# Reading expert weights in 8 KB runs per partition, with the contraction rows dealt out in another order

## The chip, the core and the metric

The kernel runs on one core of one Trainium2 chip. The metric is the device time of one execution in microseconds, as a median of runs.

## The reference, cut to what matters

One encoder layer on 2048 tokens of width 1024: attention and pooling, then a mixture of experts, then a final norm. The change touches the mixture of experts alone. There are 128 routed experts and one shared expert, each with a hidden width of 256; every token goes to 8 routed experts and to the shared one. All weights are float32.

```python
def swiglu(h, wg, wu, wd):
    return (jax.nn.silu(h @ wg) * (h @ wu)) @ wd        # wg, wu: 1024 x 256, wd: 256 x 1024

    def expert_block(args):                             # one block: 128 rows of one expert
        tok, rw, e = args
        xs = hp[tok]
        y = swiglu(xs, w_gate_e[e], w_up_e[e], w_down_e[e])
        return (y.astype(jnp.float32) * rw[:, None]).astype(hf.dtype)
```

The result of each block is added to the rows of its tokens.

## The kernel before, in words

The first part (up to about 950 us) works through 16 tiles of 128 tokens: norm, projection, attention, pooling, router. It writes the normed rows to a table in DRAM (`h2_tab`) and, for each expert, a list of (token, weight) records (`rec_tab`). A short stage then makes tables of the blocks: which records block b has, which expert it belongs to, and at which blocks the weights of the next expert are to be split. The second part is the expert loop. It has 16 blocks for the shared expert and some 200 for the routed ones. A last part norms the 2048 rows and stores them.

In the expert loop each engine has its own instruction stream, written out by hand, and they meet only at semaphores. `EW` is 6144, the columns of one expert's weights in a partition: `GUW` = 4096 for gate and up, 2048 for down. `KD` is 8, the number of 128-row slices of the contraction of 1024.

SP loads weights (`load`, L366 to L382), for one expert after another. `RAW` has two slots. For expert m, SP first waits until the gate and up weights of expert m-1 have landed (L404) and until VectorE has split those of m-2 (L406), then issues the loads of gate (L378) and up (L379). In the same way it waits for the down weights of m-1 (L409) and the split of those of m-2 (L411) and issues the load of down (L381). Each of the three loads has 1 MB. Contraction row k*128+p lies in partition p. A run that is contiguous in both DRAM and SBUF is one row: 1 KB for gate and up, which are interleaved slice by slice in `RAW`, and 4 KB for down.

ScalarE and VectorE split the weights into a float32r upper part and the remainder, six pieces of 1024 columns an expert (`upper` L577 with the copy on L586, `lower` L874 with the subtraction on L887), from `RAW` into `WS`, which also has two slots. That is done one expert ahead of TensorE.

GpSimd (POOL, L480 to L495) does three things in each block, all on one DMA queue, the software queue q0: it waits for the release of a row buffer (`xg_used`) and for the records of an earlier issue (L486), gathers the 128 rows of the block four ahead (`gather`, L461: 128 rows of 4 KB), waits for VectorE's result and for the previous addition (L488, L490), adds the finished block to `acc_tab` (L492: 128 rows of 4 KB, an accumulating DMA), and issues the load of the records of the block six ahead (`load_rec`, L478: 128 records of 8 bytes). The wait on L486 counts every record load issued so far, so that the gather of an iteration begins only when the record load issued at the end of the iteration before has landed. The hardware queue of SP is q1.

TensorE (L1073 to L1099) does, in each block b: gate and up (`parts` L1065 with `KD` = 8: 24 matmuls of 512 columns, L1068 to L1070, stationary `XR`), once the split weights and the split rows are there; 8 transposes of the rows of block b+1 (L1086, the helper's line is L956); the first half of the down projection of block b-1 (6 matmuls, stationary `HR`), once VectorE has emptied the output banks (L1088) and split the hidden rows (L1089); two transposes of the hidden block (L1097) once `hb` is there (L1095); and the other 6 down matmuls. In a transpose the data to be transposed is the stationary operand, which LDWEIGHTS reads, and the identity is the moving one.

VectorE in each block: the product `hb` (L908), the lower half of the rows (L894), the gate and up pieces of the next expert if they are due (L887), then, after `y_done` and the landing of the addition two blocks back (L914), the scaled result (L917), the lower half of the hidden rows (L921), and the down pieces. There are two result buffers, `ys`. ScalarE: silu (L608), the upper half of the rows (L590), pieces (L586), the upper half of the hidden rows (L616).

Of the kernel before, what the change touches and what calls it, by code (L numbers as in the profile page):

```python
# [6 lines left out]
P = 128  # L7
T = 2048
D = 1024
KD = D // P  # L10
# [19 lines left out]
EW = 6144  # L30
SLOTS = 2
UNROLL = 8
AHEAD = 4
# [3 lines left out]
GUW = 4096  # L37
# [73 lines left out]
def build(nc, A, out):  # L111
# [4 lines left out]
    with ctx:  # L116
# [17 lines left out]
        ident = C("ident")  # L134
# [97 lines left out]
        B = [PB[:, n, :] for n in range(8)]  # L232
# [9 lines left out]
        s = {n: sem(n) for n in names}  # L242
# [39 lines left out]
        RAW = over("RAW", SLOTS * EW, 0)  # L282
        WS = over("WS", 2 * SLOTS * EW, SLOTS * EW, f32r)
        WSf = WS[:, :].bitcast(f32)
        xg = [arena[:, 36864 + n * D:36864 + (n + 1) * D] for n in range(AHEAD)]
# [21 lines left out]
        def _(sp):  # L307
# [58 lines left out]
            def load(m, slot, part):  # L366


                at = slot * EW
                if isinstance(m, int) and m == 0:  # L370
                    src = lambda name: A[{"gate": "w_sh_gate", "up": "w_sh_up", "down": "w_sh_down"}[name]][0].rearrange("(k p) n -> p k n", p=P)
                else:
                    e = sp.value_load(tab[0:1, bass.ds(m + (9 * P - 1), 1)] if not isinstance(m, int) else tab[0:1, 9 * P + m - 1:9 * P + m],
                                      min_val=0, max_val=E - 1)
                    src = lambda name: A[f"w_{name}_e"][0, bass.ds(e, 1)].rearrange("a (k p) n -> p (a k) n", p=P)
                if part == "gu":
                    guv = RAW[:, at:at + GUW].rearrange("p (k a n) -> p k a n", k=KD, a=2)
                    sp.dma_start(guv[:, :, 0, :], src("gate")).then_inc(s["w_gu"], 16)  # L378
                    sp.dma_start(guv[:, :, 1, :], src("up")).then_inc(s["w_gu"], 16)  # L379
                else:  # L380
                    sp.dma_start(RAW[:, at + GUW:at + EW].rearrange("p (k n) -> p k n", k=2),  # L381
                                 src("down")).then_inc(s["w_dn"], 16)  # L382

            sp.wait_ge(s["p_proj"], NT)
            load(0, 0, "gu")
# [558 lines left out]
        def _(pe):  # L944
# [9 lines left out]
            def transposes(banks, src, name):  # L954
                for k in range(KD):
                    last = tr(B[banks[k // 4]][:, (k % 4) * P:(k % 4 + 1) * P], src[:, k * P:(k + 1) * P], ident)  # L956
                last.then_inc(s[name], 1)

            def step(i):
                if ok(i + 1):  # L960
                    W8(pe, "v_xn", i + 2)
# [98 lines left out]
            nblk = pe.value_load(nblk_i[0:1, 0:1], min_val=NT + 1, max_val=NT + 255)  # L1060
            pe.sem_inc(s["gu_done"], 1)
            pe.wait_ge(s["xg_r0"], 16)
            transposes((2, 3), xg[0], "xg_used")

            def parts(bank, hi, lo, w, K):  # L1065

                for k in range(K):
                    mm(bank, hi[:, k, :], w(k, 0), start=(k == 0), stop=False)  # L1068
                    mm(bank, hi[:, k, :], w(k, EW), start=False, stop=False)  # L1069
                    last = mm(bank, lo[:, k, :], w(k, 0), start=False, stop=(k == K - 1))  # L1070
                return last

            with pe.Fori(0, (256 + NT) // UNROLL) as q:  # L1073
                with pe.If(q * UNROLL < nblk + 1):
                    for n in range(UNROLL):
                        b = pe.snap(q * UNROLL + n)
                        with pe.If(b < nblk + 1):
                            l1 = pe.value_load(tab[0:1, bass.ds(b + (3 * P + 1), 1)], min_val=0, max_val=E)
                            at = pe.snap((l1 & 1) * (2 * EW))
                            pe.wait_ge(s["v_spg"], l1 + 1)  # L1080
                            pe.wait_ge(s["xgT_a"], b * 2 + 2)
                            pe.wait_ge(s["xgT_v"], b * 2 + 2)
                            parts(B[7], xh, xl, lambda k, o: WS[:, bass.ds(at + (o + k * 512), 512)], KD).then_inc(s["gu_done"], 1)
                            m = n + 1
                            pe.wait_ge(s[f"xg_r{m % AHEAD}"], (q * (UNROLL // AHEAD) + (m // AHEAD + 1)) * 16)
                            transposes((2, 3), xg[m % AHEAD], "xg_used")  # L1086
                            l0 = pe.value_load(tab[0:1, bass.ds(b + 3 * P, 1)], min_val=0, max_val=E)
                            pe.wait_ge(s["y_v"], b + 1)  # L1088
                            pe.wait_ge(s["hT_sb"], b + 1)  # L1089
                            pe.wait_ge(s["v_spd"], l0 + 1)  # L1090
                            at0 = pe.snap((l0 & 1) * (2 * EW))
                            down_w = lambda c: lambda k, o: WS[:, bass.ds(at0 + (o + GUW + k * D + c * 512), 512)]
                            parts(B[4], hh, hl, down_w(0), 2)

                            pe.wait_ge(s["h_ready"], b + 1)  # L1095
                            for k in range(2):
                                tr(B[6][:, k * P:(k + 1) * P], hb[:, k * P:(k + 1) * P], ident)  # L1097
                            parts(B[5], hh, hl, down_w(1), 2).then_inc(s["y_done"], 1)
                    settle(pe)  # L1099

# [23 lines left out]
```

## Time and profile before

| what | value |
|---|---|
| median of 3 runs | 3520.7 us (3518.12 to 3538.77) |
| profiled execution, from the first to the last instruction | 3472.9 us |
| first part, table stage and start of the loop | 0 to about 1130 us |
| routed blocks of the expert loop | about 1130 to 3400 us, 198 iterations of POOL |
| TensorE busy, share of the span | 85% |
| VectorE, ScalarE, GpSimd busy | 62%, 49%, 27% |
| bytes moved by DMA | 730 MB, mean 210 GB/s |

The profile is of one execution; its span is 47.8 us below the median of the runs, for what lies around the instructions and for the difference between executions. Busy is the time in which an engine has an instruction at work. A DMA load is cut into packets, which 16 DMA engines work off; a queue's share is the time that its packets took, as a share of 16 engines' time in the stretch.

### The profile page before, as it was taken

To read this page: it belongs to the slowest core of one execution; us is meant where nothing else is said; L and a number is where in the kernel's file an instruction comes from. 1 tells how busy PE (TensorE), PEld (TensorE's weight loads), DVE (VectorE), ACT (ScalarE), POOL (GpSimd) and SP (SyncE) were. 2 spreads that over 40 slices of the span, in tenths; PEclk is the share of its full clock that TensorE was granted. 3 is DMA by queue.
4 is the path that set the end of the run, shared out by engine and by line. 5 is a ranking of instruction groups with operands and counts; after the bars stand their busy time and mean duration, and the time that the engine had idled before them with its cause. 6 is when DMAs were issued, how large, how long until landed. Compare 5 with 4: busy or idle time off the path is not lost.

```text
span 3472.9 us, 61999 instructions
## 1 busy us (share of the span) xinstructions
PE 2951.9 (85%) x13151; PEld 2180.6 (63%) x13152; DVE 2164.1 (62%) x3443; ACT 1706.3 (49%) x2435; POOL 925.5 (27%) x794
## 2 busy tenths in 40 slices
PE   6699999999469989888798888888888888998883
PEld 2355555555358877776676767676767667776662
DVE  1146666666643665667676766666766675667774
ACT  0133333333133654656565655556556565656565
POOL 0001111111223333232333333333332323333331
PEclk9899999999779999999899999999999999999896
DMA  9501111111175887989998999899989998899997
GB/s 368 163 25 49 49 48 36 49 36 43 67 182 122 239 228 208 269 260 259 289 295 252 290 281 274 258 271 285 288 259 265 265 293 232 247 266 280 294 275 249
DMA packets 415300, 730.08 MB, mean 210 GB/s; under 512 B 31521, under 2 KB 297377, under 8 KB 414754
## 3 DMA queue, kind: packets, MB, share of 16 engines
q1 hardware_dynamic: 341314, 500.17, 42.5%
q0 software_dynamic: 73824, 228.47, 28.6%
q14 instruction: 149, 1.22, 0.1%
q8 instruction: 13, 0.21, 0.0%
HBM read 587.37 MB, written 141.19 MB: 210 GB/s over the span
## 4 chain that ended last, share of the span: by engine, by line
DMA 45%; PE 22%; issue 12%; DVE 8%; POOL 7%; POOLq 4%; ACT 2%; DVEq 0%; SPq 0%; ACTq 0%
DMA rec<-rec_tab 42%; PE PB L986 8%; POOL arena L461 3%; POOL acc_tab L492 3%; POOLq L476 3%; PE PB L951 2%; PE PB L1068 2%; PE PB L1070 2%; PE PB L1069 2%; DMA arena<-in_ada_b 1%; PE PB L1045 1%; PE PB L956 1%; DMA acc_tab<-arena,rec 1%; PE PB L970 1%; PE PB L1011 1%
## 5 line engine op out<-in xcount | busy, mean ns | idle before, releaser
L887 DVE TENSOR_TENSOR WS<-RAW,WS (+1 forms) x774 | 900.8, 1219 | 127.3 <-ACT WS L586 125.3
L586 ACT CAST WS<-RAW (+1 forms) x774 | 759.5, 1052 | 153.2 <-DMA RAW<-in_w_up_e 99.6
L1068 PE MATMUL PB<-WS,XR 128*128 x1720 | 685.6, 399 | 52.2 <-issue 46.6
L461 POOL DMA_INDIRECT arena<-h_tab,rec x219 | 255.3, 1166 | 1574.7 <-DMA rec<-rec_tab 1381.1
L1070 PE MATMUL PB<-WS,XR 128*128 x1720 | 674.7, 392 | 0.0
L1069 PE MATMUL PB<-WS,XR 128*128 x1720 | 674.0, 392 | 0.0
L917 DVE SCALAR_TENSOR_TENSOR arena<-PB,rec,G 128x512 f32<-128x512 f32 x430 | 302.5, 745 | 383.7 <-DMA acc_tab<-arena,rec 336.5
L1068 PE MATMUL PB<-WS,HR 128*128 x860 | 402.9, 468 | 154.1 <-DVE HR L921 153.0
L492 POOL DMA_INDIRECT acc_tab<-arena,rec x215 | 402.5, 1872 | 93.3 <-issue 68.4
L1068 PEld LDWEIGHTS PB<-WS,XR 128*128 128x128 f32 x1720 | 327.6, 190 | 158.7 <-issue 91.8
L1069 PEld LDWEIGHTS PB<-WS,XR 128*128 128x128 f32 x1720 | 326.7, 190 | 66.1
L1070 PEld LDWEIGHTS PB<-WS,XR 128*128 128x128 f32 x1720 | 325.4, 189 | 67.6
L1070 PE MATMUL PB<-WS,HR 128*128 x860 | 363.4, 423 | 0.0
L1069 PE MATMUL PB<-WS,HR 128*128 x860 | 361.6, 420 | 0.0
L956 PE MATMUL PB<-cst,arena 128*128 128x128 f32 x1984 | 265.4, 278 | 97.3 <-DVE arena L814 53.1
L449 POOL DMA_INDIRECT rec_tab<-recs,posi x128 | 124.6, 973 | 795.5 <-DVE recs L748 754.8
L956 PEld LDWEIGHTS PB<-cst,arena 128*128 128x128 f32 x1984 | 235.8, 143 | 138.2 <-DVE arena L814 48.4
L894 DVE TENSOR_TENSOR XR<-PB,XR 128x512 fp32r<-128x512 f32 x432 | 277.6, 684 | 65.0 <-ACT XR L590 64.8
L608 ACT ACT_TABLE_LOAD x215 | 275.8, 1283 | 74.4 <-issue 70.5
L1068 PEld LDWEIGHTS PB<-WS,HR 128*128 128x128 f32 x860 | 176.4, 205 | 193.0 <-issue 169.4
L986 PE MATMUL PB<-arena 128*128 128x512 f32 (+1 forms) x768 | 293.7, 544 | 1.5 <-ACT arena L515 1.2
L590 ACT ACTIVATE XR<-PB 128x512 fp32r<-128x512 f32 x432 | 234.6, 595 | 98.3 <-PE PB L956 98.3
(233 smaller groups left out, 2982.6 us busy)
## 6 DMA issues: line engine op xcount, KB each, us to landing
RAW<-in_w_gate_e SPq DMA_DIRECT2D x128, 1024.0 KB
RAW<-in_w_up_e SPq DMA_DIRECT2D x128, 1024.0 KB
RAW<-in_w_down_e SPq DMA_DIRECT2D x128, 1024.0 KB, 8.6
arena<-in_ada_w SPq DMA_DIRECT2D x12, 2048.0 KB, 14.3
arena<-in_x SPq DMA_DIRECT2D x32, 512.0 KB, 3.6
h_tab<-arena SPq DMA_DIRECT2D x17, 512.0 KB, 2.9
acc_tab<-arena SPq DMA_DIRECT2D x16, 512.0 KB, 2.6
out<-fa SPq DMA_DIRECT2D x16, 512.0 KB, 4.7
```

The costliest lines, as they stand in the source:

```text
L461: g.indirect_dma_start(xg[n % AHEAD], None, h2_tab, bass.IndirectOffsetOnAxis(ap=rec[:, n % UNROLL, 0:1], axis=0)).then_inc(s[f"xg_r{n % A ...
L492: g.indirect_dma_start(acc_tab, bass.IndirectOffsetOnAxis(ap=rec[:, (n - 1) % UNROLL, 0:1], axis=0), ys[(n - 1) % 2], None, compute_op=ALU ...
L586: nc.scalar.copy(to, of).then_inc(s["a_hig" if k < 4 else "a_hid"], 1)
L608: A_(eg, B[7][:, 0:F], ACT.Silu).then_inc(s["eg_done"], 1)
L887: last = V.tensor_tensor(lo, raw, hi, ALU.subtract)
L894: V.tensor_tensor(xl[:, 4 * n:4 * n + 4, :], B[2 + n].rearrange("p (a b) -> p a b", a=4), xhf[:, 4 * n:4 * n + 4, :], ALU.subtract).then_i ...
L917: last = V.scalar_tensor_tensor(out=ys[(n - 1) % 2][:, c * 512:(c + 1) * 512], in0=B[4 + c], scalar=recf[:, (n - 1) % UNROLL, 1:2], in1=G2 ...
L956: last = tr(B[banks[k // 4]][:, (k % 4) * P:(k % 4 + 1) * P], src[:, k * P:(k + 1) * P], ident)
L986: last = mm(B[4 + n][:, 0:w], xT[:, k, :], w_in[:, k, n * 512:n * 512 + w], start=(k == 0), stop=(k == KD - 1))
L1068: mm(bank, hi[:, k, :], w(k, 0), start=(k == 0), stop=False)
L1069: mm(bank, hi[:, k, :], w(k, EW), start=False, stop=False)
L1070: last = mm(bank, lo[:, k, :], w(k, 0), start=False, stop=(k == K - 1))
```

## The change

The contraction rows are dealt to partitions in another order: partition p holds rows 8p to 8p+7 of gate and up (before: rows p, 128+p, 256+p and so on), and rows 2p and 2p+1 of down. So a partition's share of each of the three weights is one contiguous run of 8 KB in DRAM. In `RAW` and `WS` gate and up no longer alternate slice by slice: all of gate comes first, then all of up. A gate and up matmul reads its 512 moving columns as two runs of 256 that lie 2048 columns apart. The split into pieces is the same code on the same number of columns.

The stationary operands must have their rows in the same order. The transposes of the gathered rows take, for slice k, columns k, k+8, k+16 and so on (a step of 32 bytes), by a new helper `row_transposes`; the two transposes of the hidden block take every other column (a step of 8 bytes).

```diff
--- before.py
+++ after.py
@@ -368,18 +368,16 @@
 
                 at = slot * EW
                 if isinstance(m, int) and m == 0:
-                    src = lambda name: A[{"gate": "w_sh_gate", "up": "w_sh_up", "down": "w_sh_down"}[name]][0].rearrange("(k p) n -> p k n", p=P)
+                    src = lambda name: A[{"gate": "w_sh_gate", "up": "w_sh_up", "down": "w_sh_down"}[name]][0].rearrange("(p k) n -> p (k n)", p=P)
                 else:
                     e = sp.value_load(tab[0:1, bass.ds(m + (9 * P - 1), 1)] if not isinstance(m, int) else tab[0:1, 9 * P + m - 1:9 * P + m],
                                       min_val=0, max_val=E - 1)
-                    src = lambda name: A[f"w_{name}_e"][0, bass.ds(e, 1)].rearrange("a (k p) n -> p (a k) n", p=P)
+                    src = lambda name: A[f"w_{name}_e"][0, bass.ds(e, 1)].rearrange("a (p k) n -> p (a k n)", p=P)
                 if part == "gu":
-                    guv = RAW[:, at:at + GUW].rearrange("p (k a n) -> p k a n", k=KD, a=2)
-                    sp.dma_start(guv[:, :, 0, :], src("gate")).then_inc(s["w_gu"], 16)
-                    sp.dma_start(guv[:, :, 1, :], src("up")).then_inc(s["w_gu"], 16)
+                    sp.dma_start(RAW[:, at:at + GUW // 2], src("gate")).then_inc(s["w_gu"], 16)
+                    sp.dma_start(RAW[:, at + GUW // 2:at + GUW], src("up")).then_inc(s["w_gu"], 16)
                 else:
-                    sp.dma_start(RAW[:, at + GUW:at + EW].rearrange("p (k n) -> p k n", k=2),
-                                 src("down")).then_inc(s["w_dn"], 16)
+                    sp.dma_start(RAW[:, at + GUW:at + EW], src("down")).then_inc(s["w_dn"], 16)
 
             sp.wait_ge(s["p_proj"], NT)
             load(0, 0, "gu")
@@ -956,6 +954,13 @@
                     last = tr(B[banks[k // 4]][:, (k % 4) * P:(k % 4 + 1) * P], src[:, k * P:(k + 1) * P], ident)
                 last.then_inc(s[name], 1)
 
+            def row_transposes(src):
+
+                cols = src.rearrange("t (p k) -> t k p", k=KD)
+                for k in range(KD):
+                    last = tr(B[2 + k // 4][:, (k % 4) * P:(k % 4 + 1) * P], cols[:, k, :], ident)
+                last.then_inc(s["xg_used"], 1)
+
             def step(i):
                 if ok(i + 1):
                     W8(pe, "v_xn", i + 2)
@@ -1060,7 +1065,7 @@
             nblk = pe.value_load(nblk_i[0:1, 0:1], min_val=NT + 1, max_val=NT + 255)
             pe.sem_inc(s["gu_done"], 1)
             pe.wait_ge(s["xg_r0"], 16)
-            transposes((2, 3), xg[0], "xg_used")
+            row_transposes(xg[0])
 
             def parts(bank, hi, lo, w, K):
 
@@ -1080,10 +1085,11 @@
                             pe.wait_ge(s["v_spg"], l1 + 1)
                             pe.wait_ge(s["xgT_a"], b * 2 + 2)
                             pe.wait_ge(s["xgT_v"], b * 2 + 2)
-                            parts(B[7], xh, xl, lambda k, o: WS[:, bass.ds(at + (o + k * 512), 512)], KD).then_inc(s["gu_done"], 1)
+                            gu_w = lambda k, o: WS[:, bass.ds(at + o, GUW)].rearrange("p (a k n) -> p k a n", a=2, k=KD)[:, k]
+                            parts(B[7].rearrange("p (a n) -> p a n", a=2), xh, xl, gu_w, KD).then_inc(s["gu_done"], 1)
                             m = n + 1
                             pe.wait_ge(s[f"xg_r{m % AHEAD}"], (q * (UNROLL // AHEAD) + (m // AHEAD + 1)) * 16)
-                            transposes((2, 3), xg[m % AHEAD], "xg_used")
+                            row_transposes(xg[m % AHEAD])
                             l0 = pe.value_load(tab[0:1, bass.ds(b + 3 * P, 1)], min_val=0, max_val=E)
                             pe.wait_ge(s["y_v"], b + 1)
                             pe.wait_ge(s["hT_sb"], b + 1)
@@ -1094,7 +1100,7 @@
 
                             pe.wait_ge(s["h_ready"], b + 1)
                             for k in range(2):
-                                tr(B[6][:, k * P:(k + 1) * P], hb[:, k * P:(k + 1) * P], ident)
+                                tr(B[6][:, k * P:(k + 1) * P], hb.rearrange("t (p k) -> t k p", k=2)[:, k, :], ident)
                             parts(B[5], hh, hl, down_w(1), 2).then_inc(s["y_done"], 1)
                     settle(pe)
```

## Rows read from the trace of the kernel before

**Rows 1.** Windows by stage: time, busy us and count per engine, granted clock, DMA share, GB/s.

```profile
280.00:1130.00 850.00, 732.59 (x3261) 469.02 (x3261) 517.64 (x1256) 278.26 (x524) 173.58 (x174) 0.92 0.23 67
1600.00:2000.00 400.00, 345.27 (x1561) 274.48 (x1560) 280.04 (x351) 242.65 (x314) 136.20 (x102) 0.93 0.96 283
2000.00:2400.00 400.00, 347.93 (x1596) 278.30 (x1594) 269.56 (x342) 239.53 (x313) 128.68 (x103) 0.95 0.93 273
```

**Rows 2.** The page, the chain that ended last, shares by line.

```profile
DMA rec<-rec_tab 42%; PE PB L986 8%; POOL arena L461 3%; POOL acc_tab L492 3%; POOLq L476 3%; PE PB L951 2%; PE PB L1068 2%; PE PB L1070 2%; PE PB L1069 2%; DMA arena<-in_ada_b 1%; PE PB L1045 1%; PE PB L956 1%; DMA acc_tab<-arena,rec 1%; PE PB L970 1%; PE PB L1011 1%
```

**Rows 3.** Waits in 1130 to 3400 us: us in total, times, longest us.

```profile
POOL arena L461 <- DMA rec<-rec_tab: 1315.5, 176, 10.1
...
DVE arena L917 <- DMA acc_tab<-arena,rec: 335.3, 88, 9.3
...
PE PB L1068 <- DVE HR L921: 153.0, 58, 8.2
...
POOL arena L461 <- DVE arena L917: 118.2, 18, 8.1
...
ACT WS L586 <- DMA RAW<-in_w_up_e: 99.6, 22, 8.2
```

**Rows 4.** Counts in 1130 to 3400 us: the record load L478 and pieces L887.

```profile
L478 POOL DMA_DIRECT2D rec<-rec_tab x198: 1165/1226/1250, 1133.2 to 3394.0; - x198
...
L887 DVE TENSOR_TENSOR WS<-RAW,WS x762: 1209/1219/1294, 1137.7 to 3382.9; - x191
```

**Rows 5.** Timeline of POOL: start us, us, what [idle before <-releaser].

```profile
2007.31 1.77 POOL L461 DMA_INDIRECT arena<-h_tab,rec  x1 [8.53 <-DMA rec<-rec_tab]
...
2019.92 1.55 POOL L461 DMA_INDIRECT arena<-h_tab,rec  x1 [7.29 <-DMA rec<-rec_tab]
...
2193.20 0.98 POOL L461 DMA_INDIRECT arena<-h_tab,rec  x1 [8.69 <-DMA rec<-rec_tab]
...
2202.09 1.04 POOL L461 DMA_INDIRECT arena<-h_tab,rec  x1 [4.91 <-DMA rec<-rec_tab]
```

**Rows 6.** Timeline of PE, the first and tenth of a run of matmuls.

```profile
2000.34 0.39 PE L1068 MATMUL PB<-WS,XR 128*128 x1
...
2002.38 0.39 PE L1068 MATMUL PB<-WS,XR 128*128 x1
```

**Rows 7.** DMA queues in 1130 to 3400 us: packets, MB, share of 16 engines.

```profile
q1 hardware_dynamic: 294144, 393.76, 52.0%
q0 software_dynamic: 63360, 207.86, 39.3%
```

**Rows 8.** DMA queues in 1994.5 to 1997.5 us, gate and up alone.

```profile
q1 hardware_dynamic: 1068, 1.08, 106.9%
```

**Rows 9.** DMA queues in 2018.5 to 2020.4 us, down alone.

```profile
q1 hardware_dynamic: 177, 0.72, 100.6%
```

**Rows 10.** DMA queues in 30.5 to 33.5 us, 8 KB rows stored to rec_tab.

```profile
q1 hardware_dynamic: 173, 1.29, 101.5%
```

**Rows 11.** DMA queues in 1998.4 to 1999.4 us, a gather beside gate and up.

```profile
q0 software_dynamic: 72, 0.29, 77.0%
q1 hardware_dynamic: 85, 0.09, 25.9%
```

**Rows 12.** DMA queues in 2002 to 2004.5 us, an addition beside down.

```profile
q0 software_dynamic: 85, 0.35, 69.5%
q1 hardware_dynamic: 88, 0.32, 34.8%
```

**Rows 13.** Weight loads of transposes (L956) and matmuls (L1070) in 1130 to 3400 us, ns min/median/max.

```profile
L956 PEld LDWEIGHTS PB<-cst,arena x1584: 138/140/148, 1134.0 to 3395.4; 128*128 128x128 f32 x198
...
L1070 PEld LDWEIGHTS PB<-WS,XR x1584: 187/188/334, 1130.4 to 3399.5; 128*128 128x128 f32 x198
```

**Rows 14.** Timeline, eight weight loads of transposes in a row.

```profile
2004.87 1.02 PEld L956 LDWEIGHTS PB<-cst,arena 128*128 128x128 f32 x8
```

## The prediction

> **What bounds the kernel now.** I read the windows by stage first. In the expert loop (from about 1130 us) the 16 DMA engines are busy 93 to 96% of the time, against 23% in the first part [rows 1]. TensorE shows busy for 345 of 400 us there, so two resources are near their limit. The change touches only this loop, so the rest (about 1200 us of the span of 3472.9) stays as it is.
>
> Next the chain that ended last. Its largest share, 42% of the span, is the landing of the record load, a transfer of 1 KB [rows 2]. Such a small thing can take 42% only because of where it stands. It is the last entry that POOL puts on queue q0, behind a gather and an addition of 512 KB each, and the next gather waits until it has landed. The waits say the same: POOL's gather waited for the record load 176 times in 198 iterations, 1315.5 us in all, and only 18 times for VectorE [rows 3]. So POOL's loop mostly bounds itself: issue, drain q0, landing, issue. The others follow: VectorE waits 335.3 us for the landing of an addition, and TensorE 153.0 us for VectorE after it [rows 3].
>
> Then the length of that loop. 198 iterations between 1133.2 and 3394.0 us make 11.48 us each [rows 4]. When few weights are coming in, an iteration takes 8.89 us (2193.20 to 2202.09); beside a whole expert's load it takes 12.61 us (2007.31 to 2019.92) [rows 5]. The excess over the short iteration is 2.59 us, 510 us over 197 iterations. 762 pieces are 127 experts [rows 4], so the excess is 4.0 us for each expert loaded. That is what the change can act on.
>
> TensorE's floor lies close below. Ten starts in a row are 2.04 us apart for nine matmuls, 0.227 us each [rows 6]; 36 of them are 8.2 us, and eight transposes take 1.0 us [rows 14], two more 0.2 us, so about 9.4 us a block. 11.48 - 9.4 is 2.1 us of slack a block, 410 us over the loop. No gain can be larger.
>
> **The change part by part.**
>
> *The loads on their own.* A load of gate, up and down gives each DMA engine 128 packets of 1 KB and 16 of 4 KB; after the change 24 of 8 KB. Time for one packet: 1 KB, 3.0 us x 16 x 1.069 / 1068 = 48 ns [rows 8]; 4 KB, 1.9 x 16 x 1.006 / 177 = 173 ns [rows 9]; 8 KB, 1.29 MB are 157 packets, 3.0 x 16 x 1.015 / 157 = 310 ns [rows 10]. The last row is of stores from SBUF to DRAM; I take it for loads as well. Alone, a load is then 128 x 48 + 16 x 173 = 8.9 us now and 24 x 310 = 7.4 us after. In the loop the 125 loads took 52.0% of 2270 us, 9.44 us each [rows 7], 6% more than alone; the same 6% gives 7.9 us. So 1.5 us less DMA work an expert, 190 us over 127 experts. It isn't 190 us of time, since POOL's loop is bound by latency: q0 needs 39.3% of 2270 us over 198 blocks, 4.5 us [rows 7], in an iteration of 8.89, and weights that come in while q0 has nothing to move cost nothing.
>
> *What a load costs POOL's loop.* Now 4.0 us for 9.44 us of work, a share of 0.42. With the same share, 7.9 us cost 3.35 us: 0.65 us less for each of 127 experts, -83 us.
>
> *Turns.* Does the share stay? Where both queues have work, they take turns packet by packet: beside a gather 72 packets of q0 against 85 of q1 [rows 11], beside an addition 85 against 88 [rows 12]. With 1 KB packets q0 gives away 48 ns a turn and has 77% of the engines' time; against 4 KB it has 69.5%, with its own packets near 0.33 us (2.5 x 16 x 0.695 / 85). Against 8 KB it gives away 310 ns a turn, and its 16 data packets an engine in each block may each wait that long. Bounds: in one short iteration q0 leaves 8.89 - 4.5 = 4.4 us in which weights cost nothing. If all of that is used, a load confined to one iteration costs 7.9 - 4.4 = 3.5 us, and one spread over 1.55 iterations (197 / 127) costs 7.9 - 6.8 = 1.1 us. If turns let weights run early so that only 3.1 us fall into q0's pauses (my estimate, 70% of the 4.4 us), it costs 4.8 us. So between 1.1 and 4.8 us, against 4.0 now: -370 to +100 us. I take 3.35 us, since 3.5 is the bound nearest to the contested iteration of rows 5, and since a queue of 128 small packets, which q0 now finds ahead of it, becomes one of 16.
>
> A rule speaks against the change here. The Trainium skill, page "DMA: Bandwidth & Descriptors", section "Queues, rings and completion order", says that an engine goes round its queues and switches only at packet boundaries, and the section "SWDGE vs HWDGE vs iDMA" prefers packets of at most 4096 B. The trace agrees on the turns [rows 11, 12]; no row shows two queues beside 8 KB packets. By the rule the 8 KB packet costs q0 its full length in each turn, which is the rival priced at +100 us below.
>
> *The transposes.* Eight weight loads a block now read with a step of 32 bytes, two with a step of 8. Before, each takes 138 to 148 ns [rows 13] and eight take 1.02 us [rows 14]. No weight load of the trace has a step. Below, nothing changes (0; nothing excludes it, and a gain has no cause). Above, I take the slowest weight load of this shape in the loop, 334 ns [rows 13], at 194 ns more: 8 x 0.194 = 1.55 us a block, 307 us over 198. I take +1.0 us a block for the eight, a little above the middle of the two ends, since a step can hardly gain anything, and nothing for the two. The floor rises from 9.4 to 10.4 us, still below POOL's iteration of about 11.1, so most of it lies in time in which TensorE would wait (2.1 us a block). It shows where TensorE catches up after a late load; I charge one block in seven, 198 / 7 x 1.0 = +28 us. If that cover is gone, it is 198 us.
>
> The Trainium skill, page "Advanced Engine Details and Errata", section "Memory Cachelines", says that SBUF has lines of 16 bytes and that full bandwidth needs at least two hits a line. A step of 32 bytes has one hit, a step of 8 has two. No run here shows it yet. By that rule eight transposes slow down and two don't; by rows 13 and 14 alone nothing is known of either.
>
> *Gate and up's moving columns* in two runs of 256: each run is contiguous and the count is the same, 0; a step in the middle could cost a few ns of 227, with an upper end of 0.02 us x 24 a block, 95 us, that I hold unlikely. *The split* (L586, L887): same pieces, 0. *SP*: the same three issues an expert; it waits for landings that come earlier. The weights arrive some 1.5 us sooner. ScalarE waited 99.6 us in 22 waits for them [rows 3]; 22 x 1.0 us of it go, -20 us.
>
> **The sum.** -83 + 28 - 20 = -75 us on the profiled execution (3472.9 to about 3398), and from the median of the runs 3520.7 - 75 = 3445 us, 2.1% faster. What is late next is still the record load.
>
> **The rivals.**
> 1. *q0 starves (slower).* Each turn costs q0 a whole 8 KB packet, and a load costs POOL's loop 4.8 us instead of 4.0: 127 x 0.8 = +100, with +28 for the transposes: 3649 us at most, and I put it at 3560 to 3649. For it: turns are packet by packet [rows 11, 12], and POOL waits for q0 in 176 of 198 iterations [rows 3]. Against: a load then finishes sooner, within one iteration. It decides once the cost of a load passes 4.0 us.
> 2. *The transposes bind (slower or level).* With +1.0 us a block fully on the path, -83 - 20 + 198: 3616 us; with half of that, 3517. For it: the DMA-bound slack is only 2.1 us a block and shrinks as loads get cheaper. Against: TensorE waits for others in most long blocks [rows 3].
> 3. *It helps more.* The excess of a load falls to 2 us: 127 x 2.0 = -254, with +50 as the floor of 10.4 us is now felt: 3317 us. For it: 4.4 us of pause in an iteration take up most of 7.9 us. Against: loads come in bursts.
> 4. *Hidden anyway.* Shorter loads are used up by longer turns, 3505 to 3540 us: loads that end sooner only wait for the split.
>
> **How the numbers follow.** The forecast (3365 to 3485) has 0.43, rival 1 has 0.17, rival 2 has 0.12 (of it 0.04 level), rival 3 has 0.10, rival 4 has 0.18. A measurement of this kernel tells about 1% (35 us) from no change. Faster by over 1%: 0.43 + 0.10 = 0.53; slower: 0.17 + 0.08 = 0.25; within 1%: 0.22. For 8 in 10 the range goes from 3350 to 3590. The forecast's own range is 3365 to 3485.
>
> **What would show the steps.** Packets of 8192 B on q1, about 49,000 in place of 294,144 in the loop, and q1's time there down from 9.44 to about 7.9 us an expert. POOL's iteration down from 11.48 to about 11.1 us, with the record load still its main releaser. Eight transposes at 2.0 us instead of 1.02 us, with the pair on L1097 unchanged. Beside a gather q0's share falls from 77% to about 35%. The forecast is wrong if POOL's iteration doesn't get shorter although q1 is cheaper (rivals 1 and 4), if TensorE's waits vanish and its block goes beyond 10.4 us (rival 2), or if the packets stay small.

## The result, and the profile after

The changed kernel takes 3617.0 us (median of 3 runs, 3601.34 to 3622.75) against 3520.7 us before. The ratio is 1.0253, with an interval of 1.0193 to 1.0312: the change makes the kernel 2.5% slower. The forecast was 2.1% faster, 3445 us, with a range of 3350 to 3590 us. Medians below are of all executions of a kernel; ratios leave out those in which the chip shows a lower granted clock and a longer time.

Its profiled execution has a span of 3615.3 us, 142.4 us more than that of before. Of these the first part took 53 us: the first gather of the loop starts at 1015.0 us, before at 962.0 us (e1 below shows that this belongs to the one execution). First the windows by stage (columns as in [rows 1]):

```profile
1600.00:2000.00 400.00, 336.69 (x1530) 269.60 (x1528) 270.60 (x342) 241.74 (x313) 123.47 (x100) 0.96 0.87 276
2000.00:2400.00 400.00, 343.98 (x1528) 278.33 (x1529) 264.27 (x336) 225.05 (x294) 121.42 (x102) 0.93 0.84 260
```

The DMA engines are less busy than before, 84 to 87% instead of 93 to 96%, and still the same stretch gets less done: TensorE shows 1530 matmuls in 1600 to 2000 us, before 1561. So work was taken off the DMA engines, and the time went up.

The queues in the expert loop say the same (1130 to 3400 us, columns as in [rows 7]):

```profile
q1 hardware_dynamic: 51407, 374.36, 42.9%
q0 software_dynamic: 61440, 201.56, 40.1%
```

q1 has 51,407 packets instead of 294,144, and its share is 42.9% instead of 52.0%. 374.36 MB are 119.0 experts of 3.146 MB, so an expert takes 0.429 x 2270 / 119.0 = 8.18 us of the 16 engines, before 9.43 us. The saving was real: 1.25 us an expert, as a difference of the two shares.

The chain that ended last has the record load at its head as before (37%, before 42%), and the landing of the addition has grown to 5% (before 1%, [rows 2]):

```profile
DMA rec<-rec_tab 37%; PE PB L991 8%; DMA acc_tab<-arena,rec 5%; POOL arena L459 3%; PE PB L1073 2%; POOL acc_tab L490 2%; PE PB L1075 2%; PE PB L1074 2%; POOLq L474 2%; PE PB L949 2%; DMA arena<-in_ada_b 1%; PE PB L1050 1%; PE PB L1016 1%; PE PB L975 1%; PE PB L961 1%
```

The waits in 1130 to 3400 us (us in total, times, longest us), to be set beside [rows 3]:

```profile
POOL arena L459 <- DMA rec<-rec_tab: 1118.3, 142, 12.8
DVE arena L915 <- DMA acc_tab<-arena,rec: 461.0, 117, 11.4
...
POOL arena L459 <- DVE arena L915: 334.6, 43, 12.0
...
PE PB L1073 <- DVE HR L919: 182.3, 79, 5.7
...
ACT WS L584 <- DMA RAW<-in_w_up_e: 45.3, 13, 5.3
```

VectorE's wait for the landing of an addition went from 335.3 to 461.0 us, and the longest single wait of POOL for a record from 10.1 to 12.8 us. In total POOL waits less for the record (1118.3 us, before 1315.5), but more for VectorE: 334.6 us in 43 waits instead of 118.2 us in 18. I read this as VectorE, held up by a late addition, being late for the next one. Both together are 7.6 us an iteration (192 gathers), before 7.2 (198). The wait of ScalarE for weights fell, from 99.6 to 45.3 us; the weights do land sooner.

The record loads and the pieces of the loop (count, ns min/median/max, first and last start), to be set beside [rows 4]. The stretch here is 1130 to 3560 us, since this loop ends later:

```profile
L476 POOL DMA_DIRECT2D rec<-rec_tab x206: 1169/1226/1255, 1132.9 to 3553.7; - x103
```

```profile
L885 DVE TENSOR_TENSOR WS<-RAW,WS x762: 1205/1216/1271, 1190.9 to 3517.3; - x191
```

2420.8 us over 205 iterations are 11.81 us each, before 11.48. 762 pieces are the same 127 experts. The excess over the short iteration of 8.89 us is 2.92 x 205 / 127 = 4.7 us an expert, before 4.0. With 0.7 x 127 that is about 90 us in the loop. The medians differ by 96 us; the spans of the two profiles differ by these 90 and the 53 of the first part.

What the two queues do when they meet is in short stretches. First a gather beside 8 KB packets (2208 to 2210 us), then an addition beside them (2970 to 2972 us); columns as in [rows 11, 12]:

```profile
q1 hardware_dynamic: 84, 0.56, 66.1%
q0 software_dynamic: 70, 0.29, 34.8%
```

```profile
q0 software_dynamic: 52, 0.21, 53.1%
q1 hardware_dynamic: 51, 0.42, 51.6%
```

The packets still alternate one for one, 84 (of which 16 are the small ones that end a load) against 70, and 51 against 52. But the share of q0 beside a gather is 34.8%, where it was 77.0% [rows 11], and beside an addition 53.1%, where it was 69.5% [rows 12].

Last, the weight loads of the transposes, with a step of 32 bytes (L961) and of 8 bytes (L1103) in the changed kernel, and eight of the former in a row on the timeline:

```profile
L961 PEld LDWEIGHTS PB<-cst,arena x1544: 186/191/208, 1130.8 to 3392.9; 128*128 128x128 f32 x193
```

```profile
L1103 PEld LDWEIGHTS PB<-cst,arena x386: 194/196/228, 1133.0 to 3394.5; 128*128 128x128 f32 x193
```

```profile
2206.18 1.09 PEld L961 LDWEIGHTS PB<-cst,arena 128*128 128x128 f32 x8
```

The former took 138 to 148 ns before [rows 13]; the latter had this row in the kernel before:

```profile
L1097 PEld LDWEIGHTS PB<-cst,arena x396: 137/140/229, 1136.3 to 3397.0; 128*128 128x128 f32 x198
```

Each got some 50 ns longer, but eight in a row take 1.09 us instead of 1.02 [rows 14].

The moving columns in two runs cost nothing. The gate and up matmuls of 1130 to 3400 us, before and after:

```profile
L1068 PE MATMUL PB<-WS,XR x1585: 387/389/791, 1130.2 to 3399.9; 128*128 x199
```

```profile
L1073 PE MATMUL PB<-WS,XR x1544: 387/389/791, 1129.6 to 3399.5; 128*128 x193
```

The median is 389 ns in both, and a piece of the split takes 1216 ns, before 1219. The mean granted clock is a little lower after the change: 0.928 to 0.934 in the executions of e1, 0.935 to 0.940 in those of the kernel before on the same chip. No run sets that apart, but a difference under 1% on an engine that isn't at the head of the chain doesn't make the 2%.

### The profile page after: what moved, and what is told of

Same layout as the page of the kernel before. It is cut to its first block, busy times and chain, and to the rows that moved or that the text cites. A ratio compares the mean times of both kernels' runs of the same rounds, so it can differ in the third digit from the quotient of the medians.

```text
span 3615.3 us, 61999 instructions
## 1 busy us (share of the span) xinstructions
PE 2996.6 (83%) x13151; PEld 2237.9 (62%) x13152; DVE 2164.1 (60%) x3443; ACT 1710.1 (47%) x2435; POOL 906.6 (25%) x794
## 4 chain that ended last, share of the span: by engine, by line
DMA 44%; PE 23%; issue 12%; DVE 7%; POOL 5%; POOLq 4%; ACT 2%; DVEq 1%; another core or an unknown queue 0%; SPq 0%; ACTq 0%
DMA rec<-rec_tab 37%; PE PB L991 8%; DMA acc_tab<-arena,rec 5%; POOL arena L459 3%; PE PB L1073 2%; POOL acc_tab L490 2%; PE PB L1075 2%; PE PB L1074 2%; POOLq L474 2%; PE PB L949 2%; DMA arena<-in_ada_b 1%; PE PB L1050 1%; PE PB L1016 1%; PE PB L975 1%; PE PB L961 1%
## 5 line engine op out<-in xcount | busy, mean ns | idle before, releaser
L459 POOL DMA_INDIRECT arena<-h_tab,rec x219 | 236.8, 1081 | 1683.4 <-DMA rec<-rec_tab 1256.2
L1073 PE MATMUL PB<-WS,HR 128*128 x860 | 408.6, 475 | 198.9 <-DVE HR L919 197.8
L1075 PE MATMUL PB<-WS,HR 128*128 x860 | 367.0, 427 | 0.0
L1074 PE MATMUL PB<-WS,HR 128*128 x860 | 365.1, 425 | 0.0
L606 ACT ACTIVATE arena<-PB 128x256 f32<-128x256 f32 x215 | 82.4, 383 | 430.8 <-PE PB L1075 426.2
L614 ACT ACTIVATE HR<-PB 128x256 fp32r<-128x256 f32 x215 | 82.5, 384 | 427.0 <-PE PB L1075 426.7
```

The source lines that it names most:

```text
L459: g.indirect_dma_start(xg[n % AHEAD], None, h2_tab, bass.IndirectOffsetOnAxis(ap=rec[:, n % UNROLL, 0:1], axis=0)).then_inc(s[f"xg_r{n % A ...
L606: A_(eg, B[7][:, 0:F], ACT.Silu).then_inc(s["eg_done"], 1)
```

## The experiments

Fifteen runs were made in four groups (e1 to e4, e5 to e8, e9 to e12, e13 to e15); each group was timed beside the kernel before on its own chip, and ratios are against that. "Iteration" below is the distance from the first to the last record load, divided by 214; it includes the 16 blocks of the shared expert.

### e1, e12: the two kernels again

No edit.

> The changed kernel once more, on the chip of the next three. Every theory expects the same time as in the first measurement, 3600 to 3625 us, 2 to 3% above before. In the first profiled execution of the changed kernel the first part ended 53 us later than before, and the loop took the other 90 us. If the 53 us belong to that one execution, the first gather at the head of the loop is back near 962 us here; if they belong to the change, it is again near 1015 us.

> The kernel before, once more, for a second profile: whether its first profiled execution (span 3472.9 us against a median of 3520.7) was a short one. If so, POOL's iteration is longer here than 11.48 us, up to 11.7 us, and the distance to the changed kernel's 12.07 us in e1 shrinks.

e1: 3578.15 us, ratio 1.0209 (1.0179 to 1.024). The time is below the band that I gave, as this chip's time for the kernel before is lower too (3499.54 us); the distance lies in the 2 to 3%. Its record loads and q1:

```profile
L476 POOL DMA_DIRECT2D rec<-rec_tab x215: 1148/1226/1255, 999.3 to 3524.5; - x108
```

```profile
q1 hardware_dynamic: 52115, 379.57, 43.5%
```

e12 (one execution, 3520.68 us):

```profile
L478 POOL DMA_DIRECT2D rec<-rec_tab x215: 1146/1226/1250, 1021.8 to 3466.8; - x108
```

```profile
q1 hardware_dynamic: 291667, 390.11, 51.4%
```

Iterations are 11.80 us (e1) and 11.43 us (e12). The two ran on different chips, so the distance is a rough one, but 0.37 x 214 = 79 us is what the medians on e1's chip differ by (3578.15 - 3499.54). The first gather starts at 960.0 us in e1, so the 53 us by which the loop began later in the first profile of the changed kernel belonged to that execution; it starts at 982.4 us in e12, so the first part, whose code is the same, varies by some tens of us. The first profile of before was a short one too: 11.31 us by the same measure (1000.8 to 3420.9 us) against 11.43 here. So a loaded expert costs 0.6 to 0.7 us more after the change, by e1 and e12 or by the first two profiles.

### e2, e3, e13: the size of the packets, with everything else as in the change

```diff
 e2: rows dealt in the new order, transposes as in the change
-src = ... .rearrange("a (p k) n -> p (a k n)", p=P)
+src = ... .rearrange("a (p k) n -> p (a k) n", p=P)
+guv = RAW[:, at:at + GUW].rearrange("p (k a n) -> p k a n", k=KD, a=2)
+sp.dma_start(guv[:, :, 0, :], src("gate")).then_inc(s["w_gu"], 16)     # 1 KB runs, up alike
+for c in range(2):
+    sp.dma_start(RAW[:, at + GUW + c * D:at + GUW + (c + 1) * D], src("down")[:, c, :])...
 ... and TensorE reads WS[:, bass.ds(at + (o + k * 512), 512)] again, gate beside up; waits on w_dn follow
 e3, e13: H = 2, H = 4 loads in place of each one
-sp.dma_start(RAW[:, at:at + GUW // 2], src("gate")).then_inc(s["w_gu"], 16)
+for c in range(H):
+    lo, hi = c * (GUW // 2 // H), (c + 1) * (GUW // 2 // H)
+    sp.dma_start(RAW[:, at + lo:at + hi], src("gate")[:, lo:hi]).then_inc(s["w_gu"], 16)
 ... up and down alike; waits on w_gu and w_dn follow
```

> The new order of rows and the strided transposes, but the packets of before: 1 KB for gate and up (interleaved in SBUF as before), 4 KB for down. Theory T (turns: q0 loses 8 KB of weights a turn): back to before, within 1% of 3520 us, POOL's iteration near 11.45 us. Rival R (the strided weight loads of the transposes cost TensorE's path): stays slow, 2 to 3% above before. Rival O (the order in which DRAM is read costs, not the size of a packet): stays slow as well.

> The changed kernel with each 8 KB run cut into two loads of 4 KB a partition, so packets of 4 KB. Theory T: a turn gives away 0.17 us instead of 0.31, so a load costs POOL's loop some 3.5 us instead of 5.0, 1.5 x 127 = 190 us less than the changed kernel: 3430 us, faster than before by 2%; at least clearly below the changed kernel. Rivals R and O: as the changed kernel, 3600 to 3625 us.

> The changed kernel with each 8 KB run cut into four loads of 2 KB a partition. If a load costs POOL's loop by turns, number times length, and a turn is always one packet: 2 KB packets (0.09 us) give away half of what 4 KB ones do, and this lands between e2 (1 KB, +0.3%) and e3 (4 KB, +3.0%), near +1 to +2%. If the cost came with the twelve DMAs an expert and their issue, or with rows read in pieces, it is as slow as e3 or slower.

e2 (1 KB for gate and up, 4 KB for down): 3509.42 us, ratio 1.0034 (1.0007 to 1.0061).

```profile
L478 POOL DMA_DIRECT2D rec<-rec_tab x215: 1161/1226/1250, 999.6 to 3475.9; - x108
```

```profile
q1 hardware_dynamic: 292530, 388.24, 51.6%
```

e13 (2 KB): 3565.43 us, ratio 1.0179 (1.0149 to 1.0209).

```profile
L482 POOL DMA_DIRECT2D rec<-rec_tab x215: 1157/1226/1250, 1002.0 to 3516.8; - x108
```

```profile
q1 hardware_dynamic: 208573, 379.80, 49.9%
```

e3 (4 KB): 3605.3 us, ratio 1.0303 (1.0276 to 1.033).

```profile
L482 POOL DMA_DIRECT2D rec<-rec_tab x215: 1157/1226/1250, 999.2 to 3548.4; - x108
```

```profile
q1 hardware_dynamic: 102816, 374.39, 47.0%
```

With the packets of before the loss is gone but for 0.3%. So it isn't the strided transposes (rival R of e2) or the rows' order in DRAM, which e2 keeps. e2 also takes back the layout of gate and up in SBUF, so by itself it doesn't tell that from the packets; the layout is ruled out by the matmuls and pieces, which take as long in it (389 ns, 1216 ns above), and by e6 below. What is left is the size of the packets. My number for e3 was wrong, though. I expected 4 KB packets to win 190 us over 8 KB ones, since a turn is half as long; they lose another 1%. e13 was added to settle whether cutting a run is harmful by itself, through more loads. It isn't: with twelve loads an expert it costs less than e3 with six, +1.8% against +3.0%, within the 1 to 2% that I gave. It ran on another chip than e2, e3 and e1.

Why is 4 KB no better than 8 KB? The turns in e3, a gather (2380 to 2382 us) and an addition (2029 to 2031 us) beside 4 KB packets:

```profile
q1 hardware_dynamic: 114, 0.41, 52.5%
q0 software_dynamic: 108, 0.41, 50.3%
```

```profile
q0 software_dynamic: 67, 0.27, 68.5%
q1 hardware_dynamic: 70, 0.27, 36.4%
```

They go one for one again. But shorter turns don't make the price of 4 KB half of that of 8 KB. I counted it from the packet records of 1130 to 3400 us. The stretch of a gather is the time from the start of its first packet of 4 KB to the start of its last. "Beside q1" are gathers during which q1 has over 15% of the 16 engines in more than 9 of 10 quarters of a microsecond. A gather with q1 quiet (under 5% throughout) takes 2.1 us in the mean in each of the four. Each row is from one profiled execution.

| run | packets of q1 | gathers beside q1: number, mean us | all gathers, mean us | all additions, mean us | q1's work an expert, us | iteration, us |
|---|---|---|---|---|---|---|
| e2 | 1 KB, 4 KB | 65, 2.36 | 2.24 | 3.63 | 9.5 | 11.57 |
| e13 | 2 KB | 68, 3.20 | 2.69 | 3.95 | 9.4 | 11.75 |
| e3 | 4 KB | 69, 3.23 | 2.66 | 3.88 | 9.0 | 11.91 |
| e1 | 8 KB | 36, 3.69 | 2.62 | 4.04 | 8.2 | 11.80 |

A single meeting with 8 KB packets costs a gather most, 1.6 us over a quiet one, but there are only half as many meetings, since q1 is done sooner. With 2 and 4 KB a meeting costs 1.1 us, twice as often. In the mean over all gathers the three come out alike, 0.4 us above e2, and so do the additions within 0.2 us. q1's own work falls only little up to 4 KB. Why 4 KB is the slowest of the three, by 0.11 us an iteration over 8 KB, is not settled by these rows.

### e4: the transposes at unit step

```diff
-cols = src.rearrange("t (p k) -> t k p", k=KD)
+cols = src.rearrange("t (k p) -> t k p", k=KD)
-tr(B[6][...], hb.rearrange("t (p k) -> t k p", k=2)[:, k, :], ident)
+tr(B[6][...], hb.rearrange("t (k p) -> t k p", k=2)[:, k, :], ident)
```

> The changed kernel with the transposes back at unit step; rows and weights no longer match, so the result is not the reference's, the work is otherwise the same. Theory T: within 0.5% of the changed kernel. Rival R: back to before, 3520 us or less.

The work is the same, but the rows no longer match the weights. 3580.78 us, ratio 1.0213 (1.0186 to 1.0241), e1 beside it 1.0209. Its weight load of a transpose is back at the old duration:

```profile
L961 PEld LDWEIGHTS PB<-cst,arena x1520: 138/140/146, 1133.9 to 3397.8; 128*128 128x128 f32 x190
```

So the step costs 50 ns of LDWEIGHTS and nothing of the kernel's time beyond the 0.3% that the intervals leave open. The rival in which the transposes bind falls.

### e5, e6: the two large transfers of q0 made small

```diff
-g.indirect_dma_start(xg[n % AHEAD], None, h2_tab, ...).then_inc(s[f"xg_r{n % AHEAD}"], 16)
+g.dma_start(xg[n % AHEAD][:, 0:64], h2_tab[0:P, 0:64]).then_inc(s[f"xg_r{n % AHEAD}"], 16)
-g.indirect_dma_start(acc_tab, ..., ys[(n - 1) % 2], None, compute_op=ALU.add).then_inc(s["added"], 16)
+g.dma_start(acc_tab[T:T + P, 0:64], ys[(n - 1) % 2][:, 0:64]).then_inc(s["added"], 16)
```

> The kernel before, with the two large transfers of the software queue made small: in the loop the gather is a plain load of 128 x 256 B and the addition a plain store of 128 x 256 B to rows that nobody uses. So the rows are wrong, and the result isn't the reference's; the weights, the split and TensorE's work are the same. Theory T (the time lies in the turns between q0 and q1): TensorE's floor of 9.3 us a block is what is left with some waits for single-block experts, POOL no longer bounds, 3100 to 3250 us.

> The same edit in the changed kernel. Theory T: without large transfers on q0 the 8 KB runs cost nothing, so this is as fast as e5 or up to 1% faster (loads land 1 to 1.5 us sooner). Rival D (8 KB runs are slower on q1's own side, or the split or TensorE pays for the new layout): it stays some 2% slower than e5.

In the loop the gather reads 256 bytes a partition of fixed rows and the addition stores as much to rows that nobody uses, so both kernels leave out the exchange of rows: the experts work on the wrong rows, and no result is added.

e5: 3275.67 us (3251.3 to 3280.93); e6: 3241.85 us (3227.87 to 3245.89). By engine, the chain that ended last, e5 first:

```profile
PE 66%; DVE 11%; issue 9%; DMA 6%; ACT 4%; DVEq 2%; SPq 1%; another core or an unknown queue 1%; ACTq 1%; POOLq 0%; POOL 0%
```

```profile
PE 67%; DVE 11%; issue 9%; DMA 5%; ACT 4%; DVEq 2%; SPq 1%; another core or an unknown queue 1%; ACTq 1%; POOLq 0%; POOL 0%
```

e5 came out some 25 us above the band that I gave. TensorE has two thirds of the chain in both, and the changed kernel is now 1.0% the faster one (3241.85 / 3275.67), with ranges that don't touch. What was a loss of 2.1% on e1's chip is a gain once q0 is nearly empty, so the 8 KB runs and the new layout cost nothing by themselves. Rival D falls.

### e7, e8: the record load just before the addition

```diff
+load_rec(b + (AHEAD + 2), (n + AHEAD + 2) % UNROLL)
 g.indirect_dma_start(acc_tab, ..., ys[(n - 1) % 2], None, compute_op=ALU.add).then_inc(s["added"], 16)
-load_rec(b + (AHEAD + 2), (n + AHEAD + 2) % UNROLL)
```

> The kernel before, with POOL's record load issued just before the addition instead of just behind it. If POOL's loop is the bound and the record load is its last link (as read from the profile of before), the record lands some 3 us sooner and the wait for the previous addition (L490) comes last: an iteration goes from 11.5 to 10.5 us, 3300 to 3400 us. If another wait of the same length stands right behind it, the time stays within 1%.

> The same edit in the changed kernel. Theory T: q0 still loses its turns to 8 KB packets, so it stays slower than e7 by 1 to 3%, and both gain. If the loss came from the record load alone (one small packet that waits behind large ones), the two would now be equal.

e7 (before with this edit): 3433.91 us, ratio 0.9779 (0.9643 to 0.9916). e8 (the change with it): 3501.24 us, ratio 0.9946 (0.9884 to 1.0007).

```profile
L478 POOL DMA_DIRECT2D rec<-rec_tab x215: 589/589/599, 1025.5 to 3379.4; - x108
```

```profile
L476 POOL DMA_DIRECT2D rec<-rec_tab x215: 587/589/599, 1005.7 to 3443.8; - x108
```

That is 11.00 and 11.39 us an iteration, so the distance between the two kernels is still 2% (3501.24 / 3433.91), as Theory T had it. The record load's own place behind the addition is not the whole of the loss. The gain in e7 is smaller than the 1.0 us an iteration and the 3300 to 3400 us that I expected. The wait of POOL ahead of the record load, which by the order of the code is now the wait for the previous addition, has 987.0 us:

```profile
POOL rec L478 <- issue: 987.0, 204, 9.4
```

The loop was still one transfer after the other: the gather waits for a record that stands behind the last gather, and the addition for the last addition.

### e9, e10, e14, e15: the record load a whole iteration ahead

```diff
 g.wait_ge(s["rec_ld"], b * 16 + 16 * (AHEAD + 1))
+load_rec(b + (AHEAD + 1), (n + AHEAD + 1) % UNROLL)
 gather(n + AHEAD)
 ...
-load_rec(b + (AHEAD + 2), (n + AHEAD + 2) % UNROLL)
```

With it, AHEAD + 1 records are loaded at the start instead of AHEAD + 2, and the waits on `rec_ld` follow.

> The kernel before, with the record load issued first of all in POOL's iteration, one block nearer (five ahead instead of six), so that the gather waits for a record load that was issued a whole iteration ago. The record is then no link of the loop at all, and only gather and addition are left. If the loop is bound by the drain of q0 (gather and addition, some 4.5 us of packets an iteration) and by TensorE's 9.4 us, an iteration goes below the 11.1 us of e7: 3350 to 3420 us, at least 1% faster than e7. If e7 already took all that there was, the same as e7, 3435 us.

> The same edit in the changed kernel. Theory T: with the record out of the loop, q0's latency counts less and the lower DMA work of 8 KB packets counts more, so the distance to e9 shrinks from the 2% of e7 and e8 towards 0 to 1%, still not faster than e9. If 8 KB packets are worse by themselves, it stays at 2%.

> 4 KB packets as in e3, with the record load issued first as in e9 and e10. If the size of a packet counts only while the record load closes POOL's loop, what is left is q1's own work for an expert, 9.0 us here against 9.5 (e9) and 8.35 (e10), so the time lies between the two, 3290 to 3350 us. If 4 KB packets are bad by themselves, it is slower than e9.

> The kernel of e10 once more, on the chip of e14, so that the two can be set side by side: 6 to 6.5% faster than before, as in e10.

| kernel | packets | us | ratio to before | iteration, us |
|---|---|---|---|---|
| e9 | 1 KB, 4 KB | 3351.55 | 0.9531 (0.947 to 0.9592) | 10.72 |
| e10 | 8 KB | 3284.0 | 0.9374 (0.9323 to 0.9425) | 10.37 |
| e14 | 4 KB | 3311.34 | 0.9454 (0.9428 to 0.9481) | 10.60 |
| e15 (as e10) | 8 KB | 3289.84 | 0.9389 (0.9362 to 0.9417) | 10.44 |

e9 and e10 ran on one chip, e14 and e15 on another. e9, e14 and e15 came out as expected. Record loads of the whole run and q1 in 1130 to 3200 us, within the loop, of e9, then of e10:

```profile
L478 POOL DMA_DIRECT2D rec<-rec_tab x215: 591/854/1240, 1006.9 to 3301.0; - x108
```

```profile
q1 hardware_dynamic: 284412, 379.98, 56.1%
```

```profile
L476 POOL DMA_DIRECT2D rec<-rec_tab x215: 593/857/1245, 994.1 to 3214.2; - x108
```

```profile
q1 hardware_dynamic: 54144, 393.76, 50.6%
```

The order has turned round: with the record out of the loop, 8 KB packets are about 2% faster than the packets of before (3284.0 / 3351.55), and 4 KB lies between the two, as expected if only q1's own work counts. I had expected the distance to shrink to 0 to 1% and the sign to stay; both were wrong. The chain that ended last of e10, by engine, has TensorE at its head, where DMA had 44% in the changed kernel:

```profile
PE 58%; DMA 13%; DVE 11%; issue 9%; ACT 4%; DVEq 2%; SPq 1%; ACTq 1%; another core or an unknown queue 0%; POOLq 0%
```

The waits of POOL in e9 and in e10 say where the meeting of the queues has gone:

```profile
POOL acc_tab L493 <- DMA acc_tab<-arena,rec: 675.3, 112, 8.4
POOL acc_tab L493 <- DVE arena L917: 310.3, 40, 13.4
```

```profile
POOL acc_tab L491 <- DMA acc_tab<-arena,rec: 875.4, 147, 9.3
...
POOL acc_tab L491 <- DVE arena L915: 213.6, 33, 9.6
```

In both the addition waits most for the one before it, in e10 longer than in e9 (875.4 against 675.3 us): the longer turns are still there. But POOL's gather is issued and on its way meanwhile, and POOL stands in wait for TensorE or VectorE otherwise, so the wait has a cover. That is read from the rows; no run tested it apart. What counts then, by that reading, is how soon the weights land. q1's work is 0.506 x 2070 / 125.2 = 8.37 us an expert in e10 against 9.61 in e9. The chain that ended last agrees, e9 first:

```profile
DMA RAW<-in_w_up_e 15%; PE PB L1068 11%; PE PB L1070 11%; PE PB L1069 11%; PE PB L986 9%; PE PB L956 4%; DVE WS L887 2%; PE PB L951 2%; ACT WS L586 2%; DMA arena<-in_ada_b 1%; PE PB L1045 1%; DMA RAW<-in_w_down_e 1%; PE PB L1097 1%; PE PB L1011 1%; PE PB L1026 1%
```

```profile
PE PB L1073 12%; PE PB L1075 12%; PE PB L1074 12%; PE PB L991 9%; DMA acc_tab<-arena,rec 6%; DMA RAW<-in_w_up_e 5%; PE PB L961 4%; DVE WS L885 2%; PE PB L949 2%; ACT WS L584 2%; PE PB L1103 2%; DMA arena<-in_ada_b 1%; PE PB L1050 1%; PE PB L1031 1%; DVE arena L915 1%
```

The landing of the up weights heads the chain of e9 with 15%, and has 5% in e10. Each is one execution.

### e11: down in 1 KB packets too

```diff
-sp.dma_start(RAW[:, at + GUW:at + EW].rearrange("p (k n) -> p k n", k=2), src("down")).then_inc(s["w_dn"], 16)
+for c in range(4):
+    sp.dma_start(RAW[...]. rearrange("p (k n) -> p k n", k=2)[:, :, c * 256:(c + 1) * 256],
+                 src("down")[:, :, c * 256:(c + 1) * 256]).then_inc(s["w_dn"], 16)
```

> The kernel before with its down weights also in 1 KB packets (four loads of 256 columns). Theory T, in the other direction: beside an addition q0 then gives away 0.05 us a turn instead of 0.17, some 0.1 to 0.3 us an iteration, while a load's own DMA work grows by 64 x 48 ns - 16 x 173 ns = 0.3 us; together 0 to 1.5% faster than before. If the length of a turn didn't matter, up to 1% slower, from the larger DMA work.

3509.23 us, ratio 0.9989 (0.9937 to 1.0042). It lies in the band of either theory and decides nothing between them. Six loads an expert, as e3 has, cost nothing here that shows beside the effect of the shorter packets.

## Why the prediction was wrong

*What bounds the kernel.* Right, and shown: POOL's loop with the record load as its last link. Taking the record out of it (e9) gives 4.7% to the kernel before, with no change to the weights.

*The loads on their own.* Right in direction, a little off in size: 8.18 us of the engines an expert instead of 7.9, so 1.25 us saved, not 1.5. The kernel as a whole is 1.0% faster where q0 is nearly empty (e5, e6).

*Turns.* This is the step that failed. I had both the mechanism (one for one, packet by packet) and the bound (up to 4.8 us an expert), and put a load's cost to POOL's loop at 3.35 us instead of 4.0, since I let the share of 0.42 of its DMA work stay. It measured 4.7 us, a share of 4.7 / 8.18 = 0.58. Instead of -83 us the term is about +90 (+79 by e1 and e12). I gave two reasons for the low value. One was the bound of 3.5 us for a load confined to one iteration, which lets the weights use all of q0's pause in it; no row had shown that they do. The other was that q0 finds 16 large packets ahead of it instead of 128 small ones. That is worth little: counted from the packet records, the first packet of a gather that has q1 beside it comes 4.2 us after the issue in e1 and 4.6 us in e12 (medians), and 1.7 us after it in both where q1 is quiet. The same count shows where the time goes: q0's stretch for a gather grows from 2.23 us (e12) to 2.62 us (e1) in the mean, that for an addition from 3.58 to 4.04 us. With q1 quiet a gather takes 2.1 us in both.

*The rule on packets.* The Trainium skill, page "DMA: Bandwidth & Descriptors", section "Queues, rings and completion order", lets an engine switch between queues at packet boundaries, and the section "SWDGE vs HWDGE vs iDMA" prefers packets of at most 4096 B. The first is what the rows show, one for one with 1, 4 and 8 KB. The second isn't borne out as a border here: 2 KB and 4 KB cost as well (e13 +1.8%, e3 +3.0%), and 8 KB costs no more than 4 KB (e1 +2.1%).

*The transposes.* The cost on the path was 0 (e4), not +28 us. The weight load got 50 ns longer with either step, but eight in a row only 0.07 us. The Trainium skill, page "Advanced Engine Details and Errata", section "Memory Cachelines", would have the step of 32 bytes slow and the step of 8 bytes free; the rows have both at some 50 ns more (191 and 196 ns, from 140), so here the measurement differs from it.

*Gate and up's moving columns.* Right: 0, the matmuls' median stays 389 ns.

*Weights that land sooner.* ScalarE's wait fell by 54 us, as foreseen and more. What that was worth to the time (-20 us in the sum) no run shows apart. With +90 and 0 in place of -83 and +28, the sum would be +70 us; +96 was measured.

*The rivals.* Rival 1, q0 starves, is what happened, with its own price (4.8 us foreseen, 4.7 measured) and a chance of 0.17 that was too low. That the two figures are so close is in part luck: 4.8 came from a guess that 70% of the pauses are used, which nothing tested, and the top of its band had 28 us for the transposes that were 0. Its band of 3560 to 3649 us holds the time. Rival 2 falls with e4. Rival 3's thought, that the gain is real where the pauses take it up, came true only with the record out of the loop (e10). My range ended at 3590 us because I gave the low value of the turns the most weight, though the bound at 4.8 was the one that the alternation in [rows 11, 12] led to.

## What to carry to other kernels

Here two DMA queues on the same engines took turns by packet, and longer packets on the bulk queue were paid by whoever waited on the other one (a gather took 3.69 us beside 8 KB packets, 2.36 us beside 1 KB ones); before packets are made larger, look at which transfer is the last link of the bounding loop. If it is a latency-bound chain on the other queue, take the small dependent transfer out of the chain first (here one moved line and the counts that follow from it, -4.7%); the larger packets then give another 2%, and the two together are the fastest kernel of this study that computes the layer (e10, e15: 0.937 to 0.939 of before).

## What the runs showed that was not expected

The cost of a packet's size isn't steady: 1 KB, 2 KB, 4 KB, 8 KB give +0.3%, +1.8%, +3.0%, +2.1%, worst in the middle. (The first has its down weights in 4 KB packets, and the second ran on another chip; each is against the kernel before on its own chip.) A meeting with longer packets costs more, but there are fewer meetings. And the sign of the 8 KB runs depends on one dependence elsewhere: +2.1% with the record load behind the addition, 2.0% faster than e9 with it ahead.

A weight load with a step of 8 bytes costs as much more as one with 32 bytes, 140 to 196 ns and 140 to 191 ns. The first part of the kernel, whose code no run changed, ended up to 53 us later in one profiled execution than in another.
